# Low halves of weights: GpSimd's subtractions of 512 and 1024 columns become subtractions of 256

## What is computed

```
h      = rmsnorm(x, norm_mix_pre)
proj   = h @ w_in                       # 1024 x 8704: RWKV | conv | attention | gates
y_a    = rwkv7_time_mix(p_rwkv, ...)    # 8 heads of 64, state updated per token
y_b    = short_conv_mix(p_conv, conv_w) # three taps, 512 channels
y_c    = dilated_attention_mix(p_attn)  # 3 groups of 4 heads, dilation 1, 4, 16
merged = sum_i sigmoid(gate_i) * (y_i @ w_branch[rows_i])   # 1280 x 1024
x      = x + rmsnorm(merged @ w_out, norm_mix_post)         # 1024 x 1024
gate, up = split(rmsnorm(x, norm_ffn_pre) @ w_ffn_in)       # 1024 x 5632
x      = x + rmsnorm((silu(gate) * up) @ w_ffn_out, norm_ffn_post)  # 2816 x 1024
```

## Time and profile before

| | |
|---|---|
| median of three runs | 943.91 us |
| the profiled execution | 944.08 us |
| its span, first to last instruction | 942.1 us |
| TensorE matmuls (PE) busy | 932.1 us, 99% of the span, 6650 instructions |
| TensorE weight loads (PEld) | 786.1 us, 83% |
| VectorE (DVE) busy | 647.7 us, 69% |
| ScalarE (ACT) busy | 430.9 us, 46% |
| GpSimd (POOL) busy | 442.9 us, 47%, 328 instructions |
| granted TensorE clock | 0.999 of full speed |
| chain that ended last | PE 52%, issue 26%, POOL 16%, DVE 4%, ACT 1% |

### The profile page before, as it was taken

One profiled execution on the slowest core, in us unless ns is written; L12 is line 12 of the kernel. 1 busy time (PEld: TensorE's weight loads), 2 busy tenths in 40 slices (PEclk: granted clock), 3 DMA queues, 4 the chain that ended last, 5 costly groups with the idle time before them and its releaser, 6 DMA issues.

```text
span 942.1 us, 16109 instructions
## 1 busy us (share of the span) xinstructions
PE 932.1 (99%) x6650; PEld 786.1 (83%) x6650; DVE 647.7 (69%) x831; ACT 430.9 (46%) x626; POOL 442.9 (47%) x328
## 2 busy tenths in 40 slices
PE   9999999999999999999999999999999999999997
PEld 7888877787887778777778888888999999988886
DVE  6777967766586756899885656988998898411114
ACT  6423515723461462336653425574556655322332
POOL 4884524344253245253245553514765565555551
PEclk9999999999999999999999999999999999999999
DMA  8323332342333265229144842286557666343312
GB/s 290 114 91 112 111 113 92 113 150 73 129 108 130 84 219 183 92 76 327 68 158 158 309 144 71 79 194 162 131 143 176 154 148 169 81 145 112 111 45 89
DMA packets 110805, 128.44 MB, mean 136 GB/s; under 512 B 3216, under 2 KB 87184, under 8 KB 110736
## 3 DMA queue, kind: packets, MB, share of 16 engines
q1 hardware_dynamic: 100224, 102.64, 33.8%
q0 software_dynamic: 2880, 10.49, 5.9%
q10 hardware_dynamic: 7632, 14.32, 4.0%
HBM read 100.70 MB, written 16.25 MB: 124 GB/s over the span
## 4 chain that ended last, share of the span: by engine, by line
PE 52%; issue 26%; POOL 16%; DVE 4%; ACT 1%; DMA 0%; POOLq 0%; DVEq 0%; ACTq 0%
POOL w_lo L741 15%; PE ps L2146 11%; PE ps L2147 11%; PE ps L2148 11%; PE ps L2692 5%; PE ps L2694 5%; PE ps L2693 5%; PE ps L2462 2%; PE ps L2522 1%; DVE x_ct L1527 1%; DVE bias_dil L1518 1%; PE ps L2497 0%; PE ps L2191 0%; PE ps L2488 0%; ACT p_buf L1125 0%
## 5 line engine op out<-in xcount | busy, mean ns | idle before, releaser
L741 POOL TENSOR_TENSOR w_lo<-w_raw,w_hi 128x512 fp32r<-128x512 f32 x220 | 317.6, 1473 | 377.8 <-ACT w_hi L890 377.4
L890 ACT CAST w_hi<-w_raw 128x2048 fp32r<-128x2048 f32 x55 | 105.0, 1909 | 135.4 <-PE ps L2148 110.3
L2278 PE MATMUL ps<-a_hi,w_hi 128*128 128x512 f32 x384 | 154.8, 403 | 0.0
L2278 PE MATMUL ps<-a_lo,w_hi 128*128 128x512 f32 x384 | 152.1, 396 | 0.0
L2278 PE MATMUL ps<-a_hi,w_lo 128*128 128x512 f32 x384 | 151.1, 393 | 0.0
L2278 PEld LDWEIGHTS ps<-a_hi,w_hi 128*128 128x128 f32 x384 | 72.1, 188 | 17.1 <-issue 1.0
L2278 PEld LDWEIGHTS ps<-a_lo,w_hi 128*128 128x128 f32 x384 | 72.2, 188 | 15.5 <-issue 1.0
L2278 PEld LDWEIGHTS ps<-a_hi,w_lo 128*128 128x128 f32 x384 | 72.1, 188 | 15.0 <-ACT xs L1051 0.2
L2063 DVE TENSOR_TENSOR f_lo<-f_all,f_hi 128x1024 fp32r<-128x1024 f32 x11 | 16.1, 1467 | 82.8 <-ACT f_hi L1325 82.8
L2692 PE MATMUL ps<-form_hi,w_hi 128*128 128x256 f32 x256 | 72.5, 283 | 0.0
L2694 PE MATMUL ps<-form_hi,w_lo 128*128 128x256 f32 x256 | 72.5, 283 | 0.0
(11 more groups left out here) (407 smaller groups left out, 2241.6 us busy)
## 6 DMA issues: line engine op xcount, KB each, us to landing
w_raw<-w_in SPq DMA_DIRECT2D x32, 1024.0 KB, 5.2
w_raw<-w_ffn_in SPq DMA_DIRECT2D x44, 512.0 KB, 5.0
spill<-spill_buf ACTq DMA_DIRECT2D x27, 512.0 KB, 3.1
w_raw<-w_ffn_out SPq DMA_DIRECT2D x11, 1024.0 KB, 4.9
late_lo<-w_raw POOLq DMA_DIRECT2D x14, 512.0 KB, 4.6
w_raw<-w_branch SPq DMA_DIRECT2D x5, 1024.0 KB, 8.1
g_ab<-spill SPq DMA_DIRECT2D x8, 512.0 KB, 4.8
w_raw<-w_out SPq DMA_DIRECT2D x4, 1024.0 KB, 7.3
```

The costliest lines, as they stand in the source:

```text
L741: g.tensor_tensor(w_lo[:, b, c], w_raw[:, b, c], w_hi[:, b, c].bitcast(F), ALU.subtract).then_inc(lo_ready, 1)
L890: s.copy(w_hi[:, b], w_raw[:, b]).then_inc(hi_ready, 1)
L2278: last = t_.matmul(ps[:, 6 + half], w[:, kt, half * P:(half + 1) * P], a, start=(kt == 0 and step == 0), stop=(kt == KT - 1 and step == 2))
```

## The change

The list of column ranges that `pieces(c0, c1)` returns cuts a stretch into ranges of `POOL_PIECE` = 256 columns. `low` goes over each quarter in two pieces, `b_low` and `t12_low` over their 1024 columns in four. The signal stays where it was: the last piece of a quarter, or of a half, carries the one increment that the single instruction had. The first slots' pieces (L749) and the masks are as before.

```diff
--- before.py
+++ after.py
@@ -70,6 +70,7 @@
     N_WIN = w_in.shape[2] // SC
     PER_T = 6
     LO_PARTS = 4
+    POOL_PIECE = 256
     S_REST = N_RWKV + NT * PER_T
     N_LEFT = N_WIN - S_REST
     N_MERGE, N_OUT, N_FIN, N_FOUT = D // SC, KT // 2, FT, FT // 2
@@ -733,12 +734,17 @@
             g = nc.gpsimd
             ch = Chain(pool, pool_chain)
             link = ch.link
+            def pieces(c0, c1):
+
+                return [slice(c, c + POOL_PIECE) for c in range(c0, c1, POOL_PIECE)]
+
             def low(n, b):
 
                 pool.wait_ge(hi_ready, n + 1)
                 for q in range(LO_PARTS):
-                    c = slice(q * SLOT // LO_PARTS, (q + 1) * SLOT // LO_PARTS)
-                    g.tensor_tensor(w_lo[:, b, c], w_raw[:, b, c], w_hi[:, b, c].bitcast(F), ALU.subtract).then_inc(lo_ready, 1)
+                    for c in pieces(q * SLOT // LO_PARTS, (q + 1) * SLOT // LO_PARTS):
+                        last = g.tensor_tensor(w_lo[:, b, c], w_raw[:, b, c], w_hi[:, b, c].bitcast(F), ALU.subtract)
+                    last.then_inc(lo_ready, 1)
 
             for i, (k0, k1) in enumerate(PIECES):
                 c = slice(k0 * SC, k1 * SC)
@@ -832,15 +838,18 @@
 
                 b = mix_buf(s)
                 pool.wait_ge(b_hi_made.sem, b_hi_made.base + s + 1)
-                g.tensor_tensor(w_lo[:, b, 0:2 * BLK], w_raw[:, b, 0:2 * BLK], w_hi[:, b, 0:2 * BLK].bitcast(F),
-                                ALU.subtract).then_inc(b_lo_made.sem, 1)
+                for c in pieces(0, 2 * BLK):
+                    last = g.tensor_tensor(w_lo[:, b, c], w_raw[:, b, c], w_hi[:, b, c].bitcast(F), ALU.subtract)
+                last.then_inc(b_lo_made.sem, 1)
 
             def t12_low(s):
 
                 b = mix_buf(s)
                 pool.wait_ge(t12_hi_made.sem, t12_hi_made.base + s + 1)
-                g.tensor_tensor(w_lo[:, b, 2 * BLK:], t12_of(s)[:], w_hi[:, b, 2 * BLK:].bitcast(F),
-                                ALU.subtract).then_inc(t12_lo_made.sem, 1)
+                for c in pieces(0, 2 * BLK):
+                    to = slice(2 * BLK + c.start, 2 * BLK + c.stop)
+                    last = g.tensor_tensor(w_lo[:, b, to], t12_of(s)[:, c], w_hi[:, b, to].bitcast(F), ALU.subtract)
+                last.then_inc(t12_lo_made.sem, 1)
 
             def late_low(s):
```

## The result

The changed kernel takes 951.39 us (median of 6 runs, 949.86 to 952.63) against 943.88 us of the kernel before in the same runs (943.32 to 944.01): a ratio of 1.0078, 95% interval 1.0068 to 1.0088, **+7.5 us**. The prediction had 946.2 and a range up to 947.6. The profiled execution took 951.12 us, 7.04 more than that of the kernel before. The runs also spread over 2.8 us, where the six of the kernel before span 0.7.

A forecast was written before the change was run, and what follows sets the result against it. TensorE was taken as the bound, so only places where it waits count: 0.44 + 0.49 - 0.3 + 1.65 = +2.28 us, giving 946.2 us beside the median of 943.91, with a range of 942.2 to 947.6.

The forecast's parts named there:

- the masks' operations: VectorE's eight attention-bias operations (L1518) each meet a 256-column piece: 5.9 us together, 6.0 before, no gain.
- slot 42: Last slot of the output projection: eight pieces end later and TensorE's weight fetch at 569 is late, +0.49 us.
- x_wide: Second half of x_wide at 585.27: shorter pieces cut VectorE's wait before TensorE's transposes, -0.3 us (0 to -0.3).
- -0.62 (-0.55): Gap at 671.16, where TensorE waits for VectorE's L2051, goes: 0.55 us come back.
- the start of the mixed slots: t12's low half of slot 1, read at 661.86, is late: TensorE stalls 2.2 us; net +1.65 (0.75 to 2.15).
- With L2013 too: Mixed slot 1's low half: if VectorE's L2013 also takes a turn between pieces, the stall is 2.7 us.
- The masks' step: Attention biases at 437.75: GpSimd's iota and the mask chain start later, TensorE loses +0.44 us (0 to 0.6).
- Where it costs nothing: Later mixed slots, RWKV slots and SP's loads have room or cover, so they add zero to the sum.
- The RWKV slots have 1.2 us or more: Slack read at 348.57; loses 0.53 and at most one or two turns of 0.45; taken as zero.
- Rival C: GpSimd becomes late in the RWKV turns as well: another 1 us or more, 947.4; chance 0.1.
- The loads on SP's queue: Loads waiting for a slot's last low half go out 0.5 to 1 us later, hidden by ScalarE's wait for TensorE.
- this price for L2031: Start of the mixed slots: VectorE's 1024-column L2031 getting in between pieces costs GpSimd 1.09 us.

The follow-up runs named there:

- experiment 11: Kernel before with the mixed slots' instructions in two pieces of 512 columns in place of one of 1024: 944.29 us (kernel before 943.83).
- experiment 12: Kernel before with mixed slots in 256 columns and VectorE waiting for mixed slot 1's low half before the third slot's sums: 944.61 us (943.83).
- experiment 13: Kernel before with slots 2, 3 and 4 alone in pieces of 256: 944.74 us (kernel before 943.92).
- experiment 14: Kernel before with slot 45 alone in pieces of 256: 945.23 us (kernel before 943.92).
- experiment 1: Changed kernel with the mixed slots' two instructions back at 1024 columns, whole slots still in 256: 949.01 us (kernel before 943.91).
- experiment 7: Kernel before, no piece resized, with GpSimd held before slot 32 until VectorE has copied the first attention values: 942.43 us (kernel before 943.92).
- experiment 3: Changed kernel with slot 45 alone back at pieces of 512: 950.21 us (kernel before 943.91).
- experiment 4: Kernel before with slot 31 alone in pieces of 256: 944.49 us (kernel before 943.91).
- experiment 8: Changed kernel with slot 45 back at 512 and the mixed slots back at 1024: 946.98 us (kernel before 943.92).
- experiment 2: Kernel before with only the mixed slots' two instructions in pieces of 256: 946.08 us (kernel before 943.91).
- experiment 9: Changed kernel with slots 2, 3, 4, 31, 42, 45 back at 512 and mixed slots 0 and 1 at 1024: 943.45 us (kernel before 943.83).

## Why the prediction was wrong
**Right.** The price of a piece and of a turn held: 5.97 us for the masks' operations (5.9 forecast), +0.52 for slot 42 (0.49), -0.38 for x_wide (-0.3), -0.62 (-0.55), and +2.80 for the start of the mixed slots, where the sum had 2.2 with two of VectorE's sums between the pieces and its own bound "With L2013 too" 2.7: three got in. Experiments 11 and 12 show the mechanism by count and by kind. The masks' step less the 0.35 that came back at 430.75 is 0.47 (0.44). That this term is so close is in part luck: 0.74 x 7 + 0.9 is 6.08 and not the 5.9 that the prediction wrote, and with 6.08 its own working gives +0.6. The terms of the sum alone, as measured, are +2.8 us, against +2.28; the other 4.5 us of the trace stand at places that the sum put at nothing.

**The step that failed** is "Where it costs nothing". Three things in it:

1. "The RWKV slots have 1.2 us or more", read from one slot in the middle, at 348.57. Slots 2 to 4, ahead of the first turn, weren't read. They had more to spare (3.7 us in slot 3), and met more: VectorE is there without a break in two-input operations, and seven boundaries took seven turns. It costs 0.8 us as a median (experiment 13), 0.9 in the changed kernel's trace and 0 to 2.3 in the others. Rival C had this mechanism, in the wrong place and with the chance of 0.1.
2. "The loads on SP's queue ... go out 0.5 to 1 us later", hidden by ScalarE's wait for TensorE. At slot 45 the load went out 3.5 us later against the rest, since VectorE's operations of 1024 columns take 1.0 and not 0.45 us from GpSimd at each boundary: a piece and its turn last 1.72 us there. The sum had this price for L2031 (1.09), and not here. And the cover was not the question: the load fell beside two DMAs that make a low half. 1.3 us alone (experiment 14), 2.0 in the changed kernel.
3. TensorE's clock was taken as given. The wait at 437.75 was costed by its length alone. When it is 2.3 to 2.6 us instead of 1.6, some executions then run 3 to 4 us at half the clock, 1.57 us more in the changed kernel's trace.

**What stays open.** Four single executions of experiments 1 and 14 took 954 to 957 us; their mean clock was 0.993 to 0.996, and what it lacks to 1, times the span, is 3.8 to 6.7 us, an estimate of a third to a half of what they are over the kernel before; no trace shows where the rest was. What decides between the two groups of experiment 13 wasn't isolated: the traces have either up to 1.0 us at 43.75 or 1.9 to 2.3 at 42.39 and 43.75 together. The number of runs doesn't settle how often the clock falls.

## What to carry to other kernels
An instruction on one engine that shares its access with another engine is also a shield: cut into pieces, it opens a boundary to each waiting operation of the other, and pays for each. Where two such engines meet ahead of a wait, have one of them wait (experiment 7) before cutting the work finer. Look for slack at every place where the work is released, the loads and DMAs behind the last piece too, not at the tightest slot of a regular stretch.

## What the runs showed of the hardware
- The granted clock after a wait differs from one execution to the next. Six traces have 2.3 to 2.6 us between two starts of matmuls at 437.75. Three show 0.50 (1.2 GHz) behind it (the changed kernel and experiment 1's executions of 948.22 and 951.28 us), three stay at 1.00 (experiments 3, 4 and 8). Of the three with 2.8 us at the start of the mixed slots (the changed kernel, experiments 2 and 3) one falls. Each fall cost 1.5 to 1.6 us. The kernel before, with 1.62 us at 437.75, stays at 1.00 in its trace.
- A GpSimd piece of 256 columns lasts 0.73 us alone (0.74 in slot 45), 1.18 when a VectorE operation of 512 columns with two SBUF inputs has got in, and 1.72 when it was one of 1024. The spacing of starts without VectorE is 0.69 us. The Trainium skill's page "SBUF — State Buffer" (Who interferes with whom) states an exclusive lock for this pair, and the traces agree: VectorE's eight operations take 1.71 us without GpSimd beside them (experiment 7) and 5.97 with it (the changed kernel).
- More instructions on GpSimd cost TensorE nothing by themselves: the 280 extra ones of experiment 9 have no cost that eleven runs can tell.
